# Six full-precision weight pieces of layer 0 turned into two-part pieces: ScalarE makes the high part and its negative, a DMA adds the weights

## The chip, the cores and the metric

One core of a Trainium2 chip runs the whole program. The metric is the device time of one execution in microseconds (us). The matrix engine is TensorE (PE in the profile; its weight loads are PEld), the elementwise engines are VectorE (DVE), ScalarE (ACT) and GpSimd (POOL), and SyncE (SP) issues most of the transfers.

## The reference

Two layers act on a sequence of 256 tokens with 1024 features, all in float32. Each layer is

```
mod = silu(c) @ w_mod[layer] + b_mod[layer]
shift, scale, gate = split(mod, 3)
hdn = rms_norm(x, norm_w) * (1 + scale) + shift
q1, k1, v1, g1, q2, k2, v2, g2 = split(hdn @ w_in[layer], 8)     # 8 x 512 columns
layer 0: y1 = diff_attention(q1, k1, v1),  y2 = dilated_attention(q2, k2, v2)
layer 1: y1 = moba_attention(q1, k1, v1),  y2 = stick_breaking_attention(q2, k2, v2)
x = x + gate * (concat(y1 * silu(g1), y2 * silu(g2)) @ w_out[layer])
```

The big products are `hdn @ w_in` (1024 x 4096) and `y @ w_out` (1024 x 1024) for each layer. `w_mod` (1024 x 3072 for each layer) is applied to one vector.

## The kernel before

**Pieces and steps.** Every 512-column group of `w_in` and `w_out` (K1, Q1, V1, K2, Q2, V2, G1, G2, O0, O1) is cut into four pieces of 256 rows, each a tile of 128 x 1024 floats (512 KB). There are 80 pieces, numbered in the order in which TensorE first needs them. TensorE's program is a list of 160 steps, 80 for a layer. A step multiplies one piece with one half of the tokens (or one half of the columns, for G1 and G2), so in layer 0 piece 20 (V2) is used in steps 40 and 41, 21 in 42 and 43, 22 in 44 and 45, 23 in 46 and 47, and pieces 24 to 27 (G1) in steps 48 to 55. `FIRST[n]` and `LAST[n]` are a piece's first and last step. After a step's projection TensorE does the attention work written down for it: scores of a pair of heads (pair 0 at step 27, then 31, 35, 39, and 46, 50, ...), transposes through the PSUM bank `turned`, products into the bank `mixed`. Each of these two banks is reused only when ACT or DVE has copied the last result out of it (`turn_act`, `mix_act`).

**Split and plain pieces.** Most pieces are split: ACT copies the loaded tile `raw` into `w_hi` as fp32r (`split_hi`, L478), DVE subtracts to get `w_lo` (`split_lo`, L751), and TensorE does three fp32r products (`mm3`: hi x hi, hi x lo, lo x hi). Pieces in the list `PLAIN` are multiplied as float32 straight from `raw`, with no work on ACT or DVE; the compiler turns each such product into two matmul instructions. A step of a split 512-column piece is thus 6 matmul instructions and one of a plain piece 4. For G1 and G2 they are 12 and 8, of 256 columns.

**Order on ACT and DVE.** Both engines walk the same 160 steps in program order. In a step g, ACT first copies what was turned or mixed in step g-1 (`take_turned`, L537 and L548; `take_mixed`, L561), then does the exponentials of the score maps (`exp_map`, L581: head 0 of a pair one step after the scores, head 1 two steps after), then the squares of finished tiles (L615) and the norm seeds (L467 to L471), and last the `split_hi` of the pieces whose `hi_at` is this step. DVE in step g does the masked logits (L853, one step after the scores), `normalise` (L865 to L876, head 1 three steps after the scores), the squares' sums (L890), `norm_tiles` (L916), then `split_lo` of the pieces with `hi_at(n) + 1 == g`, and then `take_mod` (L771), which multiplies a tile of `w_mod` with `c`; one each at steps 25, 26, 28, 29, 30, 33, 35, 37, 38, 41, 42, 43, ....

**Transfers.** SP issues the loads of pieces and `w_mod` tiles in one list, sorted by the step in which they are wanted (`FIRST[n]` for a plain piece, `hi_at(n)` for a split one). They go through a ring of seven `raw` tiles, and load i is issued when load i-7 has been used up: after `take_mod` for a `w_mod` tile, after `split_lo` for a split piece, after `LAST[n]` for a plain one. `w_hi` and `w_lo` are rings of eight slots over the split pieces alone. GpSimd makes bias maps from step 44 on and issues the loads of four late plain pieces (`HELD`) into `qT` and `kT`.

Of the kernel before, what the change touches and what calls it, by code (L numbers as in the profile page):

```python
# [9 lines left out]
ALU = mybir.AluOpType  # L10
ACT = mybir.ActivationFunctionType
# [22 lines left out]
STEPS = 80  # L34
# [33 lines left out]

HELD = (34, 37, 38, 39)
HELD_FROM = 59  # L70
PLAIN = (18, 19, 20, 21, 22, 23, 25, 26, 34, 37, 38, 39)
SPLIT = [n for n in range(len(FIRST)) if n not in PLAIN]


def split_before(n):

    i = SPLIT.index(n) - PIECES
    return SPLIT[i] if i >= 0 else None


def slot(n):
    return SPLIT.index(n) % PIECES


def split_count(n):
    return SPLIT.index(n) + 1


def done_at(layer, c, side):
# [29 lines left out]
def hi_at(n):  # L119
    if n < 12:  # L120
        return FIRST[n] - 6
    return CHANGE_HI.get(n, max(FIRST[n] - EARLY.get(n, 8), LAST[split_before(n)] + 1))


# [4 lines left out]
def lo_at(n):  # L129

    return hi_at(n) + 1


def pieces_lo(layer, g):
    return [n for n in SPLIT if lo_at(n) == STEPS * layer + g]

# [163 lines left out]
def program(nc, x, w_mod, w, a_lambda, vectors, consts, out):  # L302
    with ExitStack() as ctx:
# [6 lines left out]
        def sem(name):  # L310
            return ctx.enter_context(nc.semaphore(name))

        raw = sb("raw", [P, RAW, 2, CH])
        w_hi = sb("w_hi", [P, PIECES, 2, CH], F32R)
        w_lo = sb("w_lo", [P, PIECES, 2, CH], F32R)
# [61 lines left out]
        hi_done, lo_done, step_ok = sem("hi_done"), sem("lo_done"), sem("step_ok")  # L377
# [16 lines left out]
        y_ok, y_hi_ok, y_lo_ok = sem("y_ok"), sem("y_hi_ok"), sem("y_lo_ok")  # L394
        upd, out_ok, stored = sem("upd"), sem("out_ok"), sem("stored")
        dve_step = sem("dve_step")
        held_in = [sem(f"held_in{i}") for i in range(len(HELD))]


# [11 lines left out]
        def raw_tile(key):  # L411
            if key[0] == "w" and key[1] in HELD:
                return held[HELD.index(key[1])]
            return raw[:, place[key] % RAW, :, :]

        def wait_raw(eng, key):
            if key[0] == "w" and key[1] in HELD:
                return eng.wait_ge(held_in[HELD.index(key[1])], 16)
            eng.wait_ge(raw_full[place[key] % RAW], 16 * (place[key] // RAW + 1))

        def wait_step(eng, at):
            eng.wait_ge(step_ok, at + 1)
# [9 lines left out]
        @block.sync  # L432
        def _(sp):
            sp.dma_start(rows[:, :], vectors).then_inc(vec_in, 16)
            sp.dma_start(cst[:, C_ID:C_ID + P], consts[:, C_ID:C_ID + P]).then_inc(id_in, 16)
            sp.dma_start(xs[:, :, :], x[0].rearrange("(t p) f -> p t f", p=P)).then_inc(x_in, 16)
            for i, key in enumerate(loads):
                if i >= RAW:
                    was = loads[i - RAW]
                    if was[0] == "mod":  # L440
                        sp.wait_ge(mod_done, mods.index(was[1]) + 1)
                    else:
                        n = was[1]
                        if n in PLAIN:
                            wait_step(sp, LAST[n])
                        else:
                            sp.wait_ge(lo_done, split_count(n))
                whence = w_mod[mods.index(key[1])] if key[0] == "mod" else w[key[1]]
                sp.dma_start(raw_tile(key), whence.rearrange("p (k n) -> p k n", k=2)).then_inc(raw_full[i % RAW], 16)  # L449
                if key == ("w", 2):  # L450
                    sp.dma_start(lam, a_lambda.rearrange("a i d -> a (i d)").broadcast_to([P, 4 * HD])
                                 .rearrange("p (i d) -> p i d", i=4)).then_inc(lam_in, 16)
                if key == ("w", 11):
                    sp.dma_start(cst[:, C_TRI:], consts[:, C_TRI:]).then_inc(cst_in, 16)
            for i, (t, c) in enumerate((t, c) for t in range(2) for c in range(2)):
                sp.wait_ge(out_ok, i + 1)
                sp.dma_start(out[0, t * P:(t + 1) * P, c * CH:(c + 1) * CH],
                             xs[:, t, c * CH:(c + 1) * CH]).then_inc(stored, 16)
            sp.wait_ge(stored, 64)

        @block.scalar
        def _(act):
# [10 lines left out]
            def split_hi(n):  # L473

                wait_raw(act, ("w", n))
                if split_before(n) is not None:
                    wait_step(act, LAST[split_before(n)])
                nc.scalar.activation(w_hi[:, slot(n), :, :], raw_tile(("w", n)), ACT.Copy).then_inc(hi_done, 1)  # L478

            def h_hi(n, blocks, ts):  # L480

# [149 lines left out]
            for layer in range(LAYERS):  # L631
                for g in range(STEPS):
# [8 lines left out]
                    if at in X_SQUARE:  # L641
                        k = X_SQUARE.index(at)
# [4 lines left out]
                    for t in range(2):  # L647
# [4 lines left out]
                        if at == X_AT[t] + 1:  # L652
# [3 lines left out]
                            for kk in range(4):  # L656
                                k = 4 + kk
# [403 lines left out]

        @block.gpsimd
        def _(pool):
            pool.wait_ge(cst_in, 16)
            wait_turned(pool, ("qk", 0, Q2, 1))
            for M in range(8, 16):
                if M >= 12:
                    pool.wait_ge(logit_ok, M - 3)
                b = bias[:, M % 4, :]
                nc.gpsimd.tensor_scalar(b, dist, slope(M // 2, M % 2), 0.0, ALU.mult, ALU.add).then_inc(bias_a, 1)  # L1070
                pool.wait_ge(bias_a, M - 7)
                nc.gpsimd.tensor_tensor(b, b, dilated, ALU.add).then_inc(bias_ok, 1)


            wait_step(pool, HELD_FROM)
            for i, n in enumerate(HELD):
                nc.gpsimd.dma_start(held[i], w[n].rearrange("p (k n) -> p k n", k=2)).then_inc(held_in[i], 16)

        @block.tensor
        def _(pe):  # L1080
# [170 lines left out]
            def project(layer, g):  # L1251

                at = STEPS * layer + g
                c, p, s = STEP[layer][g]
                n = PIECE[layer, c, p]
                plain = n in PLAIN
                if plain:
                    full = raw_tile(("w", n))
                else:
                    wh, wl = w_hi[:, slot(n), :, :], w_lo[:, slot(n), :, :]  # L1260
                if layer == 0 and c == K1 and s == 0:
                    pe.wait_ge(h_ok, p + 1)
                if layer == 1 and c == K1 and p in (0, 2):
                    pe.wait_ge(h_ok, 5 + 2 * s + p // 2)
                if c >= O0 and plain:
                    pe.wait_ge(y_ok, 4 * layer + p + 1)
                elif c >= O0:
                    pe.wait_ge(y_lo_ok, 2 * layer + p + 1)
                if at == FIRST[n]:
                    if plain:  # L1270
                        wait_raw(pe, ("w", n))
                    else:
                        pe.wait_ge(lo_done, split_count(n))
                if p == 0:
                    was = before_in_bank(layer, c, s)
                    if was:
                        freed = free_act if freed_by_scalar(was[0], was[1]) else free_dve
                        if normed(*was[:2]):
                            pe.wait_ge(qn_ok, PARTS[NORMS.index(was[:2])] - 1 + s)
                        else:  # L1280
                            pe.wait_ge(freed, frees(*was))
                    if c == O1:
                        if layer == 0:
                            pe.wait_ge(logit_ok, 16)
                        else:
                            pe.wait_ge(d_a, 8)
                b = bank_of(layer, c, s)
                for a in range(2 if by_columns(layer, c) else 1):
                    for kk in range(2):
                        k = 2 * p + kk  # L1290
                        start, stop = k == 0 and a == 0, k == KB - 1
                        hb = k if c < O0 or k >= 4 else 8 + k
                        if by_columns(layer, c):
                            f = slice(2 * P * s + P * a, 2 * P * s + P * a + P)
                            i = mm(b[:, a * S:(a + 1) * S], full[:, kk, f], y[:, k, :], start, stop) if plain else mm3(b[:, a * S:(a + 1) * S], wh[:, kk, f], wl[:, kk, f],
                                    hy_hi[:, hb, :], hy_lo[:, hb, :], start, stop)
                        else:
                            ts = slice(s * P, s * P + P)
                            i = mm(b[:, :], y[:, k, ts], full[:, kk, :], start, stop) if plain else mm3(b[:, :], hy_hi[:, hb, ts], hy_lo[:, hb, ts], wh[:, kk, :], wl[:, kk, :], start, stop)
                i.then_inc(step_ok, 1)  # L1300
# [6 lines left out]
            for half in range(2):  # L1307
                for i in range(4):
                    m = V_CACT + 4 * half + i
# [107 lines left out]
```

## Time and profile before

| | |
|---|---|
| median of 3 runs | 325.1 us (324.76 to 325.23) |
| the profiled execution's own time | 324.23 us |
| its span in the profile | 322.4 us |
| granted TensorE clock, mean | 0.997 |
| TensorE busy | 299.4 us, 93% |
| VectorE busy | 235.2 us, 73% |
| ScalarE busy | 196.9 us, 61% |
| GpSimd busy | 16.2 us, 5% |
| read from HBM | 68.95 MB |

Busy times are sums over the span, and the share of a stage can be far from the mean. The time of an execution is some 1.8 us longer than the span, since it holds what lies before the first and after the last instruction.

### The profile page before, as it was taken

The numbers are of one execution on the slowest core, as the hardware profiler recorded it, in microseconds if no ns is written. First come the engines' busy times: TensorE is split into PE (matmuls) and PEld (weight loads), VectorE is DVE, ScalarE is ACT, GpSimd is POOL, SyncE is SP. The second block draws the span as 40 slices with busy tenths as digits, with TensorE's granted clock in tenths as the row PEclk, the third lists the DMA queues.
The fourth block names the chain that finished last, engine by engine and source line by source line (L and its number), as shares of the span: only waits on it lengthen the run. The fifth ranks groups of instructions, "written<-read, shape, count | busy, mean of one in ns | idle before, by whom it ended". The sixth has DMA issues, their size and how long they took to land.

```text
span 322.4 us, 4790 instructions
## 1 busy us (share of the span) xinstructions
PE 299.4 (93%) x1709; PEld 237.6 (74%) x1709; DVE 235.2 (73%) x480; ACT 196.9 (61%) x401; POOL 16.2 (5%) x24
## 2 busy tenths in 40 slices
PE   3498998999998999989999999999999999899995
PEld 2476876777555688886576888888987799798783
DVE  3898999998886697698957457989773547638633
ACT  3625568736745687998256446556664798959400
POOL 0000000000000942020000000000000000000000
PEclk9999999999999999999999999999999999999998
DMA  7999999495678958688752315679547148000011
GB/s 253 363 401 411 405 406 399 147 328 180 248 265 255 332 203 317 216 329 320 260 196 65 133 65 195 209 256 305 209 155 277 48 143 273 23 0 2 0 67 65
DMA packets 19879, 70.31 MB, mean 218 GB/s; under 512 B 2192, under 2 KB 2576, under 8 KB 19856
## 3 DMA queue, kind: packets, MB, share of 16 engines
q1 hardware_dynamic: 19280, 67.91, 58.4%
q0 software_dynamic: 576, 2.10, 1.7%
q8 instruction: 14, 0.23, 0.3%
q14 instruction: 9, 0.07, 0.1%
HBM read 68.95 MB, written 1.05 MB: 217 GB/s over the span
## 4 chain that ended last, share of the span: by engine, by line
PE 68%; DVE 12%; ACT 9%; DMA 5%; issue 3%; SPq 1%; ACTq 0%; DVEq 0%
PE proj L1082 46%; PE score L1082 13%; DMA raw<-in_w 5%; PE mixed L1082 5%; DVE raw L771 4%; DVE w_lo L751 3%; PE turned L1127 2%; ACT w_hi L478 2%; PE turned L1109 2%; DVE y L946 1%; DVE gt L938 1%; DVE probs L1021 1%; ACT y L502 1%; ACT gt L627 1%; SPq L449 1%
## 5 line engine op out<-in xcount | busy, mean ns | idle before, releaser
L751 DVE TENSOR_TENSOR w_lo<-raw,w_hi 128x1024 fp32r<-128x1024 f32 x68 | 82.3, 1222 | 14.1 <-ACT w_hi L478 13.6
L478 ACT ACTIVATE w_hi<-raw 128x1024 fp32r<-128x1024 f32 x68 | 70.6, 1050 | 17.8 <-DMA raw<-in_w 16.7
L1082 PE MATMUL proj<-w_hi,hy_hi 128*128 128x512 f32 x144 | 60.0, 417 | 4.8 <-DVE hy_lo L805 4.4
L771 DVE CUSTOM_DVE_ANT_0 raw<-raw,c_rows 128x1024 f32<-128x1024 f32 x48 | 59.0, 1251 | 0.0
L1082 PE MATMUL proj<-w_lo,hy_hi 128*128 128x512 f32 x144 | 56.9, 395 | 0.0
L1082 PE MATMUL proj<-w_hi,hy_lo 128*128 128x512 f32 x144 | 56.8, 394 | 0.0
L1082 PE MATMUL proj<-hy_hi,w_hi 128*128 128x256 f32 x176 | 52.5, 298 | 0.0
L1082 PE MATMUL proj<-hy_lo,w_hi 128*128 128x256 f32 x176 | 49.7, 283 | 0.0
L1082 PE MATMUL proj<-hy_hi,w_lo 128*128 128x256 f32 x176 | 49.7, 283 | 0.0
L1082 PEld LDWEIGHTS proj<-w_hi,hy_hi 128*128 128x128 f32 x144 | 27.5, 191 | 13.0 <-issue 3.9
L1082 PEld LDWEIGHTS proj<-hy_hi,w_hi 128*128 128x128 f32 x176 | 33.6, 191 | 2.1 <-issue 2.1
L1082 PEld LDWEIGHTS proj<-hy_lo,w_hi 128*128 128x128 f32 x176 | 33.6, 191 | 0.2 <-issue 0.2
L1082 PEld LDWEIGHTS proj<-hy_hi,w_lo 128*128 128x128 f32 x176 | 33.6, 191 | 0.0
L1082 PEld LDWEIGHTS proj<-w_hi,hy_lo 128*128 128x128 f32 x144 | 27.5, 191 | 6.1
L1082 PEld LDWEIGHTS proj<-w_lo,hy_hi 128*128 128x128 f32 x144 | 27.6, 191 | 5.4 <-issue 0.5
L581 ACT ACTIVATE probs<-logits,stat 128x128 f32<-128x128 f32 (+1 forms) x48 | 21.3, 446 | 6.7 <-DVE stat L853 6.7
L1082 PE MATMUL proj<-raw,y 128*128 128x512 f32 x48 | 22.4, 595 | 0.0
L548 ACT ACTIVATE probsT<-turned 128x384 f32<-128x384 f32 x20 | 9.7, 483 | 17.9 <-PE turned L1127 17.9
L890 DVE TENSOR_REDUCE n_ms<-sq 128x8 f32<-128x512 f32 (+1 forms) x13 | 9.4, 726 | 11.3 <-ACT sq L615 9.8
L1021 DVE SCALAR_TENSOR_TENSOR probs<-score,logits 128x384 f32<-128x384 f32 x8 | 4.1, 552 | 17.0 <-ACT logits L692 17.0
L1082 PE MATMUL score<-w_hi,hy_hi 128*128 128x512 f32 x40 | 16.1, 402 | 0.0
L1082 PE MATMUL score<-w_lo,hy_hi 128*128 128x512 f32 x40 | 15.6, 390 | 0.0
(147 smaller groups left out, 439.8 us busy)
## 6 DMA issues: line engine op xcount, KB each, us to landing
raw<-in_w SPq DMA_DIRECT2D x76, 512.0 KB, 4.7
raw<-in_w_mod SPq DMA_DIRECT2D x48, 512.0 KB, 5.7
xs<-in_x SPq DMA_DIRECT2D x1, 1024.0 KB, 5.2
qT<-in_w POOLq DMA_DIRECT2D x2, 512.0 KB, 6.5
kT<-in_w POOLq DMA_DIRECT2D x2, 512.0 KB, 8.4
out_x<-xs SPq DMA_DIRECT2D x4, 256.0 KB, 2.0
cst<-in_constants SPq DMA_DIRECT2D x1, 520.0 KB, 6.3
logits<-in_a_lambda SPq DMA_DIRECT2D x1, 128.0 KB, 12.1
```

Source lines behind the costliest of these rows:

```text
L449: sp.dma_start(raw_tile(key), whence.rearrange("p (k n) -> p k n", k=2)).then_inc(raw_full[i % RAW], 16)
L478: nc.scalar.activation(w_hi[:, slot(n), :, :], raw_tile(("w", n)), ACT.Copy).then_inc(hi_done, 1)
L502: j = nc.scalar.activation(y[:, k, :], b[:, i * S:(i + 1) * S], ACT.Identity, scale=v[:, V_A + k:V_A + k + 1], bias=v[:, V_B + k:V_B + k + 1])
L548: nc.scalar.activation(probsT[:, (2 * j + o) % 4, :], turned[:, 0:MAPW], ACT.Copy).then_inc(turn_act, 1)
L581: i = nc.scalar.activation(probs[:, M % 4, cs], logits[:, M % 2, cs], ACT.Exp, scale=-1.0, bias=st[:, tile:tile + 1], accum_out=st[:, 2 + ...
L751: nc.vector.tensor_tensor(w_lo[:, slot(n), :, :], raw_tile(("w", n)), w_hi[:, slot(n), :, :], ALU.subtract).then_inc(lo_done, 1)
L771: nc.vector.tensor_tensor_reduce(out=tile, in0=tile, in1=c_rows[:, :], scale=1.0, scalar=0.0, op0=ALU.mult, op1=ALU.add, accum_out=col(V_M ...
L890: nc.vector.reduce_sum(n_ms[:, n % 2, heads * s:heads * s + heads], src.rearrange("p (h d) -> p h d", h=heads), axis=AX.X).then_inc(ms_ok, 1)
L1021: nc.vector.scalar_tensor_tensor(out=probs[:, (2 * i + o) % 4, :], in0=score[o][:, 0:MAPW], scalar=0.0, in1=logits[:, o, :], op0=ALU.max, ...
L1082: return nc.tensor.matmul(o, a, b, start=start, stop=stop, skip_group_check=True)
L1109: i = nc.tensor.transpose(turned[:, b * P:(b + 1) * P], qn[:, s, b * P:(b + 1) * P], ident)
L1127: i = nc.tensor.transpose(turned[:, b * P:(b + 1) * P], probs[:, (2 * j + o) % 4, b * P:(b + 1) * P], ident)
```

## The change

Pieces 20 to 23 (V2) and 25, 26 (G1) of layer 0 leave `PLAIN` and become a third kind, `SUMMED`. ACT makes their `w_hi` as for a split piece, at the steps of `SUMMED_HI`, and right behind it, waiting for its own result, writes `w_lo = -w_hi` with a second pass. Then GpSimd issues a DMA that reads the piece from HBM again and adds it onto `w_lo`. DVE does nothing for these pieces. TensorE multiplies them with `mm3` after waiting for the adding DMA. SP frees their `raw` tile when `w_hi` is written. The load list is sorted by the new steps, and the slots of `w_hi` and `w_lo` move, since six more pieces pass through the ring of eight.

```
-PLAIN = (18, 19, 20, 21, 22, 23, 25, 26, 34, 37, 38, 39)
+PLAIN = (18, 19, 34, 37, 38, 39)
+
+SUMMED = (20, 21, 22, 23, 25, 26)
+SUMMED_HI = (28, 29, 31, 32, 35, 37)
 SPLIT = [n for n in range(len(FIRST)) if n not in PLAIN]
...
+def lo_count(n):
+
+    return sum(m not in SUMMED for m in SPLIT[:SPLIT.index(n) + 1])
...
+    if n in SUMMED:
+        return SUMMED_HI[SUMMED.index(n)]
...
 def pieces_lo(layer, g):
-    return [n for n in SPLIT if lo_at(n) == STEPS * layer + g]
+    return [n for n in SPLIT if n not in SUMMED and lo_at(n) == STEPS * layer + g]
...
+        neg_ok = sem("neg_ok")
+        summed_in = [sem(f"summed_in{i}") for i in range(len(SUMMED))]
...
                         if n in PLAIN:
                             wait_step(sp, LAST[n])
+                        elif n in SUMMED:
+                            sp.wait_ge(hi_done, split_count(n))
                         else:
-                            sp.wait_ge(lo_done, split_count(n))
+                            sp.wait_ge(lo_done, lo_count(n))
...
                 nc.scalar.activation(w_hi[:, slot(n), :, :], raw_tile(("w", n)), ACT.Copy).then_inc(hi_done, 1)
+                if n in SUMMED:
+                    act.wait_ge(hi_done, split_count(n))
+                    nc.scalar.activation(w_lo[:, slot(n), :, :], w_hi[:, slot(n), :, :], ACT.Copy,
+                                         scale=-1.0).then_inc(neg_ok, 1)
...
         @block.gpsimd
         def _(pool):
+            for i, n in enumerate(SUMMED):
+                pool.wait_ge(neg_ok, i + 1)
+                nc.gpsimd.dma_start(w_lo[:, slot(n), :, :], w[n].rearrange("p (k n) -> p k n", k=2),
+                                    accum_op=ALU.add).then_inc(summed_in[i], 16)
             pool.wait_ge(cst_in, 16)
...
                     if plain:
                         wait_raw(pe, ("w", n))
+                    elif n in SUMMED:
+                        pe.wait_ge(summed_in[SUMMED.index(n)], 16)
                     else:
-                        pe.wait_ge(lo_done, split_count(n))
+                        pe.wait_ge(lo_done, lo_count(n))
```

## Rows read from the trace of the kernel before

**Rows 1.** The profile's page: busy time of each engine; the chain by engine.
```profile
PE 299.4 (93%) x1709; PEld 237.6 (74%) x1709; DVE 235.2 (73%) x480; ACT 196.9 (61%) x401; POOL 16.2 (5%) x24
...
PE 68%; DVE 12%; ACT 9%; DMA 5%; issue 3%; SPq 1%; ACTq 0%; DVEq 0%
```

**Rows 2.** Busy time by stretch: us, busy of each engine, clock, DMA share, GB/s.
```profile
66.00:80.56 14.56, 14.56 (x79) 11.24 (x78) 12.87 (x41) 7.39 (x25) 0.00 (x0) 1.00 0.72 248
80.56:113.36 32.80, 31.93 (x147) 18.83 (x145) 24.13 (x66) 19.75 (x54) 8.64 (x12) 1.00 0.79 277
```

**Rows 3.** The chain of waits, stretch 66 to 126 us: start, us, what.
```profile
73.17 2.77 PE proj L1082 x12
...
85.70 3.44 PE proj L1082 x8
...
108.74 6.51 PE proj L1082 x36
...
116.58 1.73 PE proj L1082 x8
```

**Rows 4.** Timeline of ACT, steps 31 to 37: start, us, what, idle before.
```profile
70.52 0.60 ACT L615 ACTIVATE sq<-proj 128x512 f32<-128x512 f32 x1 [1.77 <-PE proj L1082]
73.21 0.49 ACT L548 ACTIVATE probsT<-turned 128x384 f32<-128x384 f32 x1 [2.09 <-PE turned L1127]
...
75.74 0.19 ACT L581 ACTIVATION_READ_ACCUMULATOR probs<-logits,stat 128x1 f32 x1
...
77.17 1.06 ACT L478 ACTIVATE w_hi<-raw 128x1024 fp32r<-128x1024 f32 x1
80.76 0.49 ACT L548 ACTIVATE probsT<-turned 128x384 f32<-128x384 f32 x1 [2.53 <-PE turned L1127]
82.58 0.40 ACT L581 ACTIVATE probs<-logits,stat 128x128 f32<-128x128 f32 x1 [1.33 <-DVE stat L853]
...
83.48 0.67 ACT L537 ACTIVATE kT<-turned,v 128x512 f32<-128x512 f32 x1
84.05 0.39 ACT L581 ACTIVATE probs<-logits,stat 128x128 f32<-128x128 f32 x1
```

**Rows 5.** Timeline of ACT at 113 us: one pass behind another.
```profile
113.36 1.04 ACT L478 ACTIVATE w_hi<-raw 128x1024 fp32r<-128x1024 f32 x1
114.30 1.48 ACT L590 ACTIVATE probs<-probs,stat 128x128 f32<-128x128 f32 x4
```

**Rows 6.** Timeline of DVE, steps 34 to 36.
```profile
76.90 0.16 DVE L870 RECIPROCAL stat<-stat 128x2 f32<-128x2 f32 x1
...
77.35 0.75 DVE L876 SCALAR_TENSOR_TENSOR probs<-probs,stat 128x128 f32<-128x128 f32 x2
...
81.91 0.29 DVE L853 CUSTOM_DVE_ANT_0 logits<-score,cst 128x128 f32<-128x128 f32 x1
```

**Rows 7.** Timeline of PE, steps 35 to 38.
```profile
80.17 0.55 PE L1127 MATMUL turned<-cst,probs 128*128 128x128 f32 x3
...
82.28 0.60 PE L1109 MATMUL turned<-cst,qn 128*128 128x128 f32 x4
...
85.54 3.60 PE L1082 MATMUL proj<-raw,y 128*128 128x512 f32 x8
```

**Rows 8.** Issue of piece 19's load; landing times of loads, 75 to 150 us.
```profile
72.04 0.33 SPq L449 DMA_DIRECT2D raw<-in_w  x1
...
DMA to landing us min/median/max: 3.2/4.4/7.9
...
kT<-in_w POOLq DMA_DIRECT2D x2, 512.0 KB, 8.4
```

**Rows 9.** Busy time in G2's stage; timelines of ACT and PE at step 53.
```profile
124.00:146.00 22.00, 20.22 (x167) 17.93 (x166) 16.63 (x42) 20.59 (x51) 2.30 (x4) 1.00 0.82 308
...
121.07 0.67 ACT L542 ACTIVATE y<-turned,v 128x512 f32<-128x512 f32 x1
...
122.37 0.60 PE L1119 MATMUL turned<-cst,gt 128*128 128x128 f32 x4
```

## The prediction

> **What bounds the kernel now.** I read the page first. TensorE is busy for 93% of the span and 68% of the chain that ended last is its own [rows 1], so a matmul saved on PE is worth its time wherever PE does not wait. Then I read the stretches. The six pieces are multiplied in steps 40 to 53, from about 90 to 122.4 us; the new ACT work is put at steps 28 to 37, from 66 to 84 us. In that earlier stretch PE is busy without a gap while ACT works for 7.39 of 14.56 us [rows 2]. The reader should see that this half-idle ACT is waiting for PE and DVE at fixed points, so that its free time is in the wrong places as much as in the right ones. Third I read the chain of waits for the price of a step, and last the timelines of ACT, DVE, PE and SP around steps 31 to 38, because what has to be known there is the order of the queues, which no sum shows.
>
> **What a step saves.** Two steps of split 512-column pieces take 2.77 us (12 instructions), two plain ones 3.44 us (8 instructions) [rows 3]. A split step is therefore 1.385 us and a plain one 1.72, and a V2 step saves 0.335 us. The eight V2 steps (40 to 47) give 2.7 us. A plain step of G1 takes 1.73 us; steps 47 to 50 take 6.51 together, of which 1.72 and 1.8 are the plain steps 47 and 50 (the second with 0.1 of hand-over to the scores behind it), so a split G1 step is about 1.49 [rows 3]. That saves 0.24 us in each of the steps 50 to 53, 1.0 us in all. PE's part is 3.7 us if nothing takes its place.
>
> **What of that ACT takes back later.** From the scores of step 46 on, ACT is nearly full: in G2's stage it works 20.59 of 22 us [rows 9]. It starts on the first subln tile at 121.07, after unbroken work, and PE can turn the second one into the same bank only when that copy ends, at 121.7; it does so at 122.37 today [rows 9]. So PE can come 0.6 us earlier here and no more, where steps 47 and 50 to 53 would give 1.3. What remains is 7 x 0.335 = 2.35 for steps 40 to 46 and 0.6, or 2.95 us. The bounds are 2.35 (ACT passes on nothing) and 3.7.
>
> **What the conversions cost before step 38.** One `w_hi` pass lasts 1.04 us and the next instruction may start 0.94 after it [rows 5]. The second pass waits for the first to end, so a piece costs ACT 1.06 + 0.94 and some 0.05 for the semaphore, 2.05 us; nothing in this trace shows a negating copy, and the same shape and engine give the price. Six pieces are 12.3 us. Followed through the queue:
>
> Steps 28, 29, 31 and 32 put four pieces (8.2 us) ahead of the exponentials of pair 1, head 1. ACT's idle time on that way is 1.77 + 2.09 us, and these exponentials end at 75.84 today (start of the last accumulator read 75.74 plus 0.1) [rows 4]. They end at 75.84 + 8.2 - 3.86 = 80.2. The scores of pair 0 are not hurt: head 1's exponentials end 2.1 us later, and the 1.1 us of `normalise` behind them still end before PE wants the map.
>
> DVE normalises pair 1 right behind: from 76.90 to 78.1 today [rows 6], so to 81.4. PE wants to turn this map at 80.17 [rows 7]. **First stall, 1.2 us.**
>
> ACT goes on with the norm seeds, a copy out of `mixed` and `w_hi` of piece 24, which today run from 75.84 to 78.1 [rows 4], so to 82.5; then piece 25 of step 35 (2.05), to 84.5. Only then does it copy the turned map of pair 1, which it started at 80.76 today. That copy frees the bank `turned` at 85.0. PE wants the bank for K2 at 82.28 [rows 7]. **The stall grows to 2.7 us in all.**
>
> DVE does `norm_tiles`, `split_lo` of piece 24, `take_mod` of step 35 and then the logits of pair 2: 5.0 us from 76.90 to 81.91 [rows 6]. Begun 3.3 us later, at 80.2, this brings the logits to 85.2 and those of head 0 to 85.8. ACT's exponentials (0.9) and the copy of K2's first half (0.57) follow [rows 4], so `turned` is free again at 87.3 to 87.4; PE wants it at 84.43, after one more step of 1.72. **The stall is 3.0 us** when step 38, today at 85.54, may start at 88.5.
>
> The load of piece 19, plain and needed in that step, is the last term. Today it is issued at 72.04 [rows 8], 13.5 us ahead, because its ring slot falls free at the `take_mod` of step 30. In the new list six pieces come earlier, and its slot is that of the `w_mod` tile of step 35, used up at 85.2. A load lands 3.2 to 7.9 us after its issue, 4.4 in the median [rows 8]: at 89.7 with the median, 1.2 us after PE could start. The range is 0 to 4.7. **By step 38 PE is 4.2 us late.** From there ACT has only pieces 26 and 27 in front of it, and its 13 idle us between 80.56 and 113.36 [rows 2] let it catch up before the turn of step 39; I add 0.2 for the shorter steps behind which the Q2 norm chain (43, 44) has to hide. The bounds of this part are 3.0 and 8.0; below 3.0 only if my order on ACT is wrong, and then down to 1.2, the first stall alone.
>
> **The other parts.** DVE loses nothing and gains nothing: plain pieces never used it. The adding DMAs follow the negating passes, which by the queue above end at about 70, 73, 75.5, 79, 84.5 and 90.3 us, and are read at steps 40 to 52, from 94 to 120 us. The nearest rows are the loads that GpSimd issues, 8.4 us to landing [rows 8]; even twice that is hidden for each. GpSimd does nothing else before step 44. They add 3.1 MB to a stretch that moves 248 GB/s with a DMA share of 0.72 [rows 2], beside 3.1 MB of loads pulled forward. I take their effect on pieces 18 and 19 as nothing beyond the median above; the upper bound is the 7.9 us. The ring tiles that come free sooner in steps 40 to 53 feed loads that already arrive in time, since PE waits for none today. POOL, PEld and the clock (1.00 in all these stretches [rows 2]) stay as they are.
>
> One rule speaks against the change and is not in the sum. In the Trainium skill, "Collectives: The Full Stack" (Part 3, the bandwidth ceiling) says that a DMA add is slowed by its two source reads, and so runs at about half the rate of a copy. No row here has an adding DMA. As an estimate by that page, each one would take the DMA engines as long as two loads.
>
> **The sum.** 4.2 + 0.2 - 2.95 = +1.45 us, on the profiled execution 324.23 + 1.45 = 325.7. The median of the runs shown is 0.9 above that execution, so 325.1 + 1.5 = 326.6 us.
>
> **The rivals.**
> *The gain comes through.* ACT's idle time absorbs the conversions, with only the first stall, 1.2 us, left: 325.1 + 1.2 - 2.95 to -3.7 is 322.6 to 323.4. For it speaks that ACT is half idle from 66 to 80 us; against it, that the order above puts 6.15 us of conversions between scores and exponentials of the same pair. This decides if the turn of K2 starts less than 1 us later after the turn of step 35 than now.
> *Piece 19 is in time.* The load lands in 3.2 us: 3.0 + 0.2 - 2.95 is +0.25, 325.4 us, no change. It needs a quiet queue, but an adding DMA (piece 25) and the load of piece 27 are issued within a microsecond of it.
> *The transfers become the bound.* Six adds and six earlier loads share the DMA engines in 68 to 92 us; piece 18 (issued about 74.5, needed at 81.7) and piece 19 land late together. With 7.9 us to landing for piece 19: 325.1 + 7.7 + 0.2 - 2.95 = 330.1, with 6 us 328.2. The stretch 80 to 113 already has a share of 0.79 [rows 2]. The half rate that the Trainium skill ("Collectives: The Full Stack") gives for adds would lead here; no row shows it.
> *The split products are no cheaper.* If three fp32r products took as long as one float32 product, the change would only cost: 325.1 + 4.2 + 0.2 = 329.5. For it speaks that a split step has 6 instructions and a plain one 4; the chain's durations [rows 3] speak plainly against it.
>
> **Numbers.** Forecast, 325.8 to 328.4: 0.45. Piece 19 in time, 324.5 to 325.7: 0.18. Gain comes through, below 324.4: 0.24. Transfers the bound, above 328.4: 0.11. No cheaper: 0.02. A difference under 0.2% (0.65 us) is about what a measurement here can't tell from none. Faster is 0.24, same 0.18, slower 0.58. The range 322.8 to 329.3 reaches into both outer rivals and leaves out their far ends, where ACT's order costs nothing (below 322.8, 0.07) or piece 19 lands after 7 us and more (above 329.3, 0.08, with the last rival); the forecast's own is 325.8 to 328.4.
>
> **What would show it.** PE's two-step stretch at V2 should fall from 3.44 to 2.77 us. PE's turn of pair 1's map should be released by DVE's L876, the turn of K2 by ACT's copy L548 and L537, and step 38 by the DMA of `raw`, issued behind the `take_mod` of step 35. ACT should be without a gap from 67 to about 92 us. I am wrong if PE has no idle time between 80 and 92 us, if piece 19's load is issued well before 85, or if G1's steps bring 0.24 each with ACT no obstacle.

## The result, and the profile after

The changed kernel takes 333.96 us in the median (333.43 to 335.36, 4 runs) against 324.93 us for the kernel before in the same session (324.39 to 325.23, 4 runs). The ratio is 1.0294 [1.0273, 1.0314]: 9 us slower. The forecast of 326.6 us had the direction and missed the size by 7.4 us; 333.96 is also above the range. The profiled execution has a span of 331.9 us, where the one before had 322.4.

The page of the changed kernel, to be laid beside [rows 1]. In the slices, each of 8.3 us, PEclk is the granted clock in tenths:

```profile
span 331.9 us, 4878 instructions
...
PE 297.7 (90%) x1741; PEld 241.0 (73%) x1741; DVE 235.4 (71%) x480; ACT 208.3 (63%) x413; POOL 21.5 (6%) x30
...
PEclk9997999999589999999999999999999999999999
...
q1 hardware_dynamic: 19280, 67.91, 56.6%
q0 software_dynamic: 1440, 5.24, 6.5%
...
PE 64%; ACT 12%; DMA 10%; DVE 9%; issue 4%; SPq 1%; ACTq 0%; DVEq 0%
...
w_lo<-in_w POOLq DMA_DIRECT2D x6, 512.0 KB, 9.6
```

PE is busy for 1.7 us less than before (297.7 against 299.4), and yet the span grows by 9.5. The DMA's share of the chain has doubled, from 5 to 10%, and two slices of the clock, at about 83 to 99 us, have fallen to 0.5 and 0.8. Both point to one place. (The 0.7 at 25 to 33 us, behind a wait of 2.66 us for DVE, costs nothing: the turn that PE began at 60.08 us before begins at 60.12.) PE's timeline there:

```profile
81.36 0.55 PE L1149 MATMUL turned<-cst,probs 128*128 128x128 f32 x3 [0.95 <-DVE probs L894]
90.56 3.53 PE L1104 MATMUL proj<-raw,y 128*128 128x512 f32 x4 [8.66 <-DMA raw<-in_w]
93.93 0.60 PE L1131 MATMUL turned<-cst,qn 128*128 128x128 f32 x4
```

The first line is the predicted turn of pair 1's map (before at 80.17 [rows 7]), 1.2 us late. The second is step 36, the first of the plain piece 18: PE waits 8.66 us for that load. The third shows that the step then took 3.37 us (90.56 to 93.93) where a plain step takes 1.72. The windows say why, and what the DMA engines did meanwhile (columns as in [rows 2]):

```profile
66.00:78.00 12.00, 12.00 (x63) 9.31 (x60) 8.45 (x31) 10.96 (x22) 2.77 (x3) 1.00 0.97 298
78.00:82.00 4.00, 2.95 (x18) 1.77 (x16) 2.84 (x9) 3.90 (x12) 0.88 (x1) 1.00 1.06 278
82.00:86.00 4.00, 0.00 (x0) 0.00 (x0) 4.00 (x12) 2.30 (x4) 0.00 (x0) 0.68 1.06 278
86.00:90.00 4.00, 0.00 (x0) 0.00 (x0) 1.88 (x6) 1.29 (x6) 0.87 (x1) 0.50 1.03 284
90.00:94.00 4.00, 3.44 (x5) 1.47 (x6) 0.00 (x0) 0.00 (x0) 0.00 (x0) 0.54 1.06 285
94.00:98.00 4.00, 4.00 (x21) 2.58 (x20) 1.77 (x5) 3.40 (x7) 0.00 (x0) 1.00 1.03 418
```

The last two columns are to be read together. From 66 us on all 16 DMA engines are full (shares of 0.97 to 1.06, where [rows 2] have 0.72 and 0.79), but while adds are in flight they move only 278 to 298 GB/s; when the fifth is through (it lands at 94.7) they move 418 GB/s at the same share. Full engines that move less: the adds cost engine time that their bytes don't show. The clock column is 0.50 in the second half of the wait and 0.54 in the step behind it, which is the 1.2 GHz level, and 1.00 (2.4 GHz) from 94 us on.

The chain of waits from 72 to 94 us, where before it ran through PE (the 2.77 and 3.44 us pieces of [rows 3]):

```profile
73.38 0.96 ACT w_hi L492
74.33 0.02 issue
74.35 16.17 DMA raw<-in_w
90.52 0.04 issue
90.56 3.53 PE proj L1104 x4
```

Piece 18 is issued at 74.35, as the prediction had it (about 74.5), and takes 16.17 us to land, where a load took 3.2 to 7.9 before [rows 8]. POOL's timeline shows what ran beside it, and the tile's view gives the landing times:

```profile
70.29 1.03 POOL L1084 DMA_DIRECT2D w_lo<-in_w  x1 [69.84 <-ACT w_lo L495]
73.21 0.88 POOL L1084 DMA_DIRECT2D w_lo<-in_w  x1 [1.88 <-ACT w_lo L495]
75.71 0.86 POOL L1084 DMA_DIRECT2D w_lo<-in_w  x1 [1.62 <-ACT w_lo L495]
79.48 0.88 POOL L1084 DMA_DIRECT2D w_lo<-in_w  x1 [2.92 <-ACT w_lo L495]
86.33 0.87 POOL L1084 DMA_DIRECT2D w_lo<-in_w  x1 [5.97 <-ACT w_lo L495]
```
```profile
L1084 POOL DMA_DIRECT2D w_lo<-in_w x6: 857/870/1033, 70.3 to 98.5; - x6
...
DMA to landing us min/median/max: 8.4/9.6/11.2
```

The adds themselves land in 8.4 to 11.2 us, long before their readers want them. It is the ordinary load beside them that comes late.

**Where the 9.5 us are.** The scores of pair 3 (step 39) and of step 46 are good milestones: 89.07 and 107.81 before, 100.72 and 117.28 after. At the first PE is 11.65 us behind: 0.95 for the turn, 8.66 for the load, 1.65 for the clock, and 0.4 for an earlier offset and hand-overs. Between the two it takes 16.56 us instead of 18.74, so the split products give back 2.2. From step 46's scores to the end it is 214.6 us in both (322.4 - 107.81 and 331.9 - 117.28): the split G1 steps bring nothing.

### The profile page after: what moved, and what is told of

Its sections match the earlier page's. It is cut to its first block, busy times and chain, and to the rows that moved or that the text cites. A ratio compares the mean times of both kernels' runs of the same rounds, so it can differ in the third digit from the quotient of the medians.

```text
span 331.9 us, 4878 instructions
## 1 busy us (share of the span) xinstructions
PE 297.7 (90%) x1741; PEld 241.0 (73%) x1741; DVE 235.4 (71%) x480; ACT 208.3 (63%) x413; POOL 21.5 (6%) x30
## 3 DMA queue, kind: packets, MB, share of 16 engines
q1 hardware_dynamic: 19280, 67.91, 56.6%
## 4 chain that ended last, share of the span: by engine, by line
PE 64%; ACT 12%; DMA 10%; DVE 9%; issue 4%; SPq 1%; ACTq 0%; DVEq 0%
PE proj L1104 43%; PE score L1104 13%; DMA raw<-in_w 10%; PE mixed L1104 5%; ACT w_hi L492 2%; PE turned L1131 2%; DVE raw L789 2%; PE turned L1149 2%; DVE w_lo L769 1%; ACT probs L599 1%; DVE y L964 1%; DVE gt L956 1%; DVE logits L871 1%; DVE probs L1039 1%; ACT y L520 1%
## 5 line engine op out<-in xcount | busy, mean ns | idle before, releaser
L492 ACT ACTIVATE w_hi<-raw 128x1024 fp32r<-128x1024 f32 x74 | 76.8, 1050 | 18.4 <-DMA raw<-in_w 17.1
L1104 PE MATMUL proj<-w_hi,hy_hi 128*128 128x512 f32 x160 | 66.7, 417 | 5.3 <-DVE hy_lo L823 5.0
L1104 PE MATMUL proj<-w_hi,hy_lo 128*128 128x512 f32 x160 | 63.1, 394 | 0.0
L1104 PE MATMUL proj<-w_lo,hy_hi 128*128 128x512 f32 x160 | 63.1, 394 | 0.0
L1104 PE MATMUL proj<-hy_hi,w_hi 128*128 128x256 f32 x192 | 56.8, 296 | 0.0
L1104 PE MATMUL proj<-hy_lo,w_hi 128*128 128x256 f32 x192 | 54.2, 282 | 0.0
L1104 PE MATMUL proj<-hy_hi,w_lo 128*128 128x256 f32 x192 | 54.2, 282 | 0.0
L1104 PEld LDWEIGHTS proj<-w_hi,hy_hi 128*128 128x128 f32 x160 | 30.5, 190 | 13.6 <-issue 4.3
L1104 PE MATMUL proj<-raw,y 128*128 128x512 f32 x16 | 9.0, 704 | 8.7 <-DMA raw<-in_w 8.7
L1104 PE MATMUL score<-w_hi,hy_lo 128*128 128x512 f32 x40 | 15.6, 390 | 0.0
```

Source lines behind the costliest of these rows:

```text
L1104: return nc.tensor.matmul(o, a, b, start=start, stop=stop, skip_group_check=True)
```

## The experiments

The question was which of these holds the loss: what an adding DMA costs beyond a copy, the mere bytes of six more reads, ACT's queue, the order of the loads, or the clock. The median of the kernel before was 324.89 us beside the first four experiments, 324.5 beside the next four and 324.19 beside the last two; each ratio is against its own. The diffs are against the changed kernel unless said otherwise.

**1. The same DMAs as plain copies.** The low part is then the whole weight, and the kernel leaves out the subtraction.
```diff
-  nc.gpsimd.dma_start(w_lo[...], w[n]..., accum_op=ALU.add).then_inc(summed_in[i], 16)
+  nc.gpsimd.dma_start(w_lo[...], w[n]...).then_inc(summed_in[i], 16)
```


> The changed kernel with the six adding DMAs turned into plain copies of the same bytes from the same queue to the same place (the low part then holds the whole weight, so the sum of the products is another one). Theory A, an add occupies the DMA engines about twice as long as a copy, and that work is what makes piece 18 land 16.2 us after its issue: the work outstanding between 68.6 and 90.5 us falls from about 3.1 MB of loads + 2 x 2.1 MB of adds to 3.1 + 2.1 MB, 13 us at 400 GB/s, so piece 18 lands at 81 to 84 us, PE waits 0 to 2 us instead of 8.7, and the median is 325.5 to 328.5 us. Rival B, it is the number of transfers and bytes, whatever they do: piece 18 still lands after 88 us, and the median stays above 332 us. Rival C, the passes on ACT are the cost: no change from the changed kernel, 334 us.

Measured: 329.77 us, ratio 1.0148 [1.0106, 1.019], above the expected 325.5 to 328.5 and below rival B's 332. PE's wait for piece 18 is halved, not gone:

```profile
86.67 3.78 PE L1103 MATMUL proj<-raw,y 128*128 128x512 f32 x4 [4.02 <-DMA raw<-in_w]
```

The DMA engines are as full as with the adds, but now move 410 GB/s (columns as in [rows 2]):

```profile
82.00:86.00 4.00, 0.55 (x3) 0.31 (x3) 3.93 (x9) 3.34 (x5) 0.53 (x1) 0.89 1.07 410
```

The page gives the cost of a DMA in engine time:

```profile
q0 software_dynamic: 1440, 5.24, 4.3%
```

That queue also carries the four held loads, which the kernel before has alone at 1.7% of 322.4 us: 5.5 us of all 16 engines, 1.37 each. Six copies take 4.3% of 328.8 less 5.5, so 1.44 us each; six adds take 6.5% of 331.9 less 5.5, so 2.68 us each. An add costs 1.9 times a copy of the same 512 KB. So about half of the wait is what the adds cost beyond copies (8.66 against 4.02 us), and the other half comes with six plain copies in their place. The expectation that took the dearer add for the whole cause was wrong.

The rule that the prediction had set beside its sum stands in the Trainium skill, "Collectives: The Full Stack", Part 3, the bandwidth ceiling: the reducing step of a collective needs two source reads for its DMA add and runs at about half the rate of the copying one. The page speaks of rings of cores, not of a load; this trace agrees with the ratio, 2.68 against 1.44 us. That a second read is the reason here too was not tried.

**2. No adding DMAs at all.** PE waits for the negative high part alone, and the kernel leaves out the weights' part of `w_lo`.
```diff
-  nc.gpsimd.dma_start(w_lo[...], w[n]..., accum_op=ALU.add).then_inc(summed_in[i], 16)
...
-  pe.wait_ge(summed_in[SUMMED.index(n)], 16)
+  pe.wait_ge(neg_ok, SUMMED.index(n) + 1)
```


> The changed kernel without the six adding DMAs: PE waits for the negating pass instead (the low part is then the negative high part alone). Theory A: the wait for piece 18 is gone. What remains is the ACT queue: first stall 1.0 us, 2.7 by the turn of K2, 3.0 by step 38, then the wait for piece 19, 0 to 1.5 us, and against it 2.2 to 2.95 us saved at steps 40 to 53: 325.4 to 327.0 us. Rival B, the six loads pulled forward are themselves too much before step 36: PE still waits more than 2 us for piece 18, median above 328 us. Rival C, ACT: 334 us.

Measured: 326.49 us, ratio 1.0049 [1.0032, 1.0066]; the span is 323.9. PE's idle times:

```profile
81.43 0.55 PE L1147 MATMUL turned<-cst,probs 128*128 128x128 f32 x3 [0.95 <-DVE probs L894]
...
84.84 0.63 PE L1129 MATMUL turned<-cst,qn 128*128 128x128 f32 x4 [1.15 <-ACT probsT L566]
...
87.56 0.63 PE L1129 MATMUL turned<-cst,qn 128*128 128x128 f32 x4 [0.37 <-ACT kT L555]
...
88.69 3.62 PE L1102 MATMUL proj<-raw,y 128*128 128x512 f32 x8
```

These are the three stalls that the prediction worked out, at the predicted instructions: 1.2, 2.7 and 3.0 us had been forecast as running totals, and PE starts step 38 at 88.69, which had been put at 88.5. There is no wait for a load: piece 19 is issued at 85.30 (predicted 85.2) and is there 3.3 us later, at 88.6, just as PE wants it. So the conversions on ACT cost 3.2 us at the scores of pair 3 (92.24 against 89.07), the loads pulled forward cost nothing without the adds, and 1.6 us come back by the scores of step 46 (109.42 against 107.81). The transfers of the adds are worth 333.96 - 326.49 = 7.5 us.

**3. The adds held back until steps 34, 36, 38, 40, 41 and 42,** so that piece 18 goes ahead of most of them.
```diff
   pool.wait_ge(neg_ok, i + 1)
+  wait_step(pool, ADD_FROM[i])
```


> The changed kernel with the same work, but GpSimd issues the adds only when PE has done steps 34, 36, 38, 40, 41 and 42. Theory A: piece 18 (issued at 74.4) lands by 80 us as no add is in flight, PE's wait of 8.7 us and the 1.65 us lost to the lower clock behind it go away; piece 19 (issued at 85.2) then shares the queues with two adds and lands 5 to 8 us later, a wait of 1.5 to 4.5 us: 327 to 330 us. Rival D, the adds move the stall to where they are read: PE waits for an add at step 40 or 42 by 2 us or more, and the median stays above 330 us. Rival C, ACT: 334 us.

Measured: 331.94 us, ratio 1.0229 [1.0188, 1.0269], above the expected 327 to 330, which had no term for the clock. Piece 18 is now in time and piece 19, 6.9 us to landing, is not:

```profile
92.01 6.65 PE L1106 MATMUL proj<-raw,y 128*128 128x512 f32 x8 [3.42 <-DMA raw<-in_w]
```

Two plain steps take 6.65 us, where [rows 3] have 3.44 for them: the clock is 0.50 to 0.64 between 90 and 98 us. The wait costs 3.4 us and the clock behind it 3.2. The DMA share is 1.02 to 1.11 from 86 to 98 us: the surplus of work was moved, and only in part taken away.

**4. The six pieces split in the ordinary way,** at the same steps, the low part by DVE, without an adding DMA.
```diff
-SUMMED = (20, 21, 22, 23, 25, 26)
-SUMMED_HI = (28, 29, 31, 32, 35, 37)
+SUMMED = ()
+SUMMED_HI = ()
...
+ 20: 28, 21: 29, 22: 31, 23: 32, 25: 35, 26: 37   (added to CHANGE_HI)
```


> The six pieces as ordinary split pieces at the same steps: one ACT pass each, the low part by DVE one step later, no add. Theory A plus my account of the ACT queue: ACT has four passes (3.9 us) instead of eight ahead of the exponentials of pair 1, head 1, which its idle 3.9 us absorb, but DVE gets six passes of 1.14 us, three of them before its normalise of step 34; DVE has only 2.3 us idle from 64 to 82 us. First stall 0.5 to 2 us, piece 19 issued 2 to 4 us late but landing in time or by 1 us late, gain at steps 40 to 53 of 2.2 to 2.95: 323.5 to 326 us. Rival C (ACT passes were the whole cost, six instead of twelve): about half the loss, 329 us. Rival E (DVE becomes the bound): above 327 us.

Measured: 326.78 us, ratio 1.006 [1.0043, 1.0076].

```profile
82.77 0.55 PE L1150 MATMUL turned<-cst,probs 128*128 128x128 f32 x3 [2.40 <-DVE probs L895]
```

DVE is the queue that is late here: PE waits 2.40 us for it, the clock averages 0.79 from 82 to 90 us, and by the scores of pair 3 PE is 4.5 us behind (93.57). Both the wait (expected 0.5 to 2 us) and the time (323.5 to 326) came out higher than expected. It is still 7 us faster than the changed kernel. Against experiment 2, where ACT makes both passes and nothing is added, it is 0.3 us slower, and the two intervals overlap: to spare DVE the low parts was worth no more than that, and was paid for with 7.5 us of transfers.

**5. The adds alone.** The kernel before, plus six adding DMAs into slots of `w_lo` that are idle and are overwritten before their next use, at steps 28 to 37. The diff is against the kernel before.
```diff
+ EXTRA = ((20, 2, 28), (21, 3, 29), (22, 4, 31), (23, 5, 32), (25, 6, 35), (26, 7, 37))
...
+ for i, (n, s, at) in enumerate(EXTRA):
+     wait_step(pool, at)
+     nc.gpsimd.dma_start(w_lo[:, s, :, :], w[n]..., accum_op=ALU.add).then_inc(extra_in[i], 16)
```


> The kernel before, with nothing changed but six adding DMAs of the same six pieces, issued by GpSimd when PE has done steps 28, 29, 31, 32, 35 and 37, into w_lo slots that hold nothing then (DVE waits for them before it writes the slot). Order and steps of all other loads are those of before, with pieces 18 and 19 issued at 68.6 and 72.0 us. Theory A': the adds cost only where a load wanted soon stands behind them; piece 18 lands before the first adds take effect and piece 19 (needed at 85.5) has 13 us, so PE waits 0 to 1 us and the median is 324.9 to 326.5 us. Rival G: the volume of the adds alone (six times two loads' work) starves PE wherever the loads stand: a wait of more than 3 us on a load, median above 328.

Measured: 330.99 us, ratio 1.0217 [1.0197, 1.0237]. Nothing else of the change is in this kernel, and it has 6.5 us of the loss, where 0 to 1.5 were expected; rival G, the volume of the adds alone, was right. Pieces 18 and 19, issued early, are in time; the wait is at piece 20, issued at 82.5 and 11.7 us to landing:

```profile
94.27 5.40 PE L1091 MATMUL proj<-raw,y 128*128 128x512 f32 x8 [3.68 <-DMA raw<-in_w]
```

Up to the scores of pair 3 this kernel is level with the one before (89.18 against 89.07); 3.68 us of wait and 2.0 us of a slower pair of steps (5.40 against 3.44) are all of the 5.7 us by which its span is longer.

**6. Only the V2 pieces;** 25 and 26 stay plain, so four adds.
```diff
-PLAIN = (18, 19, 34, 37, 38, 39)
+PLAIN = (18, 19, 25, 26, 34, 37, 38, 39)
-SUMMED = (20, 21, 22, 23, 25, 26)
+SUMMED = (20, 21, 22, 23)
-SUMMED_HI = (28, 29, 31, 32, 35, 37)
+SUMMED_HI = (28, 29, 31, 32)
```


> The changed kernel with only the four V2 pieces (20 to 23) as summed pieces, and the two G1 pieces (25, 26) plain as before. If the two G1 pieces bring nothing at steps 50 to 53 because ACT sets the pace from step 46 on (PE in the second run gained 1.6 us from scores of step 39 to those of 46 and lost 0 from there to step 53), nothing is lost by leaving them out, and two ACT passes of 2.05 us, two adds and two early loads go: piece 18 stands one load earlier (issued at 73.2) and the wait for it falls from 8.7 to 3 to 6 us; the second and third stall (copy of the turned map behind piece 25) go. 328 to 331 us. If the G1 steps did bring their 1.0 us: the time between the turns of steps 50 and 53 grows by 1 us against the changed kernel. Rival B', the adds of pieces 20 to 23 alone already hold piece 18 to 90 us: median 333 or more.

Measured: 330.87 us, ratio 1.0203 [1.0184, 1.0222], in the expected range (328 to 331).

```profile
87.00 3.78 PE L1104 MATMUL proj<-raw,y 128*128 128x512 f32 x4 [4.14 <-DMA raw<-in_w]
```

Dropping the fifth and sixth piece takes 4.5 us off the wait for piece 18; with them go the fifth add and the load of piece 25 ahead of piece 18, and what each is worth was not tried apart. It loses nothing in G1: from the scores of step 46 (114.49) to the end it takes 329.0 - 114.49 = 214.5 us, with plain G1 steps, where the changed kernel takes 214.6 with split ones.

**7. The four V2 pieces split late,** at steps 34, 35, 38 and 39, in the ordinary way, with 24 and 27 moved behind them. Against the kernel before:
```diff
-PLAIN = (18, 19, 20, 21, 22, 23, 25, 26, 34, 37, 38, 39)
+PLAIN = (18, 19, 25, 26, 34, 37, 38, 39)
...
+ 20: 34, 21: 35, 22: 38, 23: 39, 24: 41, 27: 42   (added to CHANGE_HI)
```


> A candidate from these readings: the kernel before with the four V2 pieces as ordinary split pieces (low part by DVE, no add), converted where ACT and DVE have idle time: 20 at step 34, 21 at 35, 22 at 38, 23 at 39, and pieces 24 and 27, which stood at 34 and 38, at 41 and 42; G1 stays plain. Theory A: no adds, no load order that puts six pieces ahead of 18 and 19 (issued at about 70 and 78 us); PE loses 0 to 0.5 us before step 40 and keeps 1.6 to 2.0 us of V2: 323.0 to 324.3 us against 324.9. Rival E (DVE is late): DVE gets three more passes between steps 39 and 45 and PE is 2 us faster there, 5.4 us against 5.9 us idle; if it comes late with the logits of step 47, the gain is given back: 324.9 to 326.

Measured: 324.65 us, ratio 0.9998 [0.998, 1.0015], where 323.0 to 324.3 had been expected. This trace starts 0.6 us later than that of before (its first scores are at 65.88 against 65.24). With this taken off, no stall has come up by the scores of pair 3 and PE is 1.8 us ahead at step 46 (106.69). Then:

```profile
115.95 0.55 PE L1128 MATMUL turned<-cst,probs 128*128 128x128 f32 x3 [1.29 <-ACT probs L591]
```

PE waits for a map that ACT scales, and at the end all 1.8 us are gone: from the scores of step 46 it takes 216.3 us here (323.0 - 106.69), 214.6 in the kernel before. A gain on PE counts up to the place where the chain of ACT and DVE begins to set the pace; pieces 24 and 27, moved into it, are the likely load, which was not tried apart.

**8. Piece 18's load moved forward** in the order of the loads.
```diff
-later = [(FIRST[n] if n in PLAIN else hi_at(n), 1, ("w", n)) ...
+later = [(34 if n == 18 else FIRST[n] if n in PLAIN else hi_at(n), 1, ("w", n)) ...
```


> The changed kernel with one load moved: piece 18 is issued ahead of pieces 24 and 25 and one w_mod tile, at about 70 us instead of 74.4. Work and adds are the same. Theory A (the DMA engines have more work than time between 69 and 92 us): piece 18 lands in time, before 81 us, but pieces 24 and 25 land later, 25 at 86 to 89 us, and ACT, which converts 25 ahead of its copy of the turned map, holds PE at the turn of K2 (step 36) instead; the loss moves and shrinks little: 330 to 334 us. Rival F, only the place of piece 18 in the queue is wrong: PE waits for nothing but the three ACT stalls (2.5 us) and piece 19: 326.5 to 328.5 us.

Measured: 334.23 us, ratio 1.0295 [1.0275, 1.0315], the same as the change (expected were 330 to 334). Piece 18 is in time, but now ACT waits for the pieces it has to convert, and PE behind ACT:

```profile
84.99 1.06 ACT L492 ACTIVATE w_hi<-raw 128x1024 fp32r<-128x1024 f32 x1 [2.91 <-DMA raw<-in_w]
...
88.80 1.06 ACT L492 ACTIVATE w_hi<-raw 128x1024 fp32r<-128x1024 f32 x1 [2.75 <-DMA raw<-in_w]
```
```profile
91.47 1.08 PE L1131 MATMUL turned<-cst,qn 128*128 128x128 f32 x4 [7.03 <-ACT probsT L566]
```

So it was not the place of piece 18 in the list: with the DMA engines full (a share of 1.02 to 1.08 from 80 to 96 us), this order only changes who waits.

**9. Experiment 7, with the low parts of 20 to 23 made by GpSimd.** Against the kernel before, beside the edits of experiment 7:
```diff
+BY_POOL = (20, 21, 22, 23)
...
+ for n in BY_POOL:
+     pool.wait_ge(hi_done, split_count(n))
+     nc.gpsimd.tensor_tensor(w_lo[:, slot(n), :, :], raw_tile(("w", n)),
+                             w_hi[:, slot(n), :, :], ALU.subtract).then_inc(pool_lo, 1)
```


> The late-split candidate (V2 pieces 20 to 23 split at steps 34, 35, 38, 39) with their low part made by GpSimd, idle there, instead of DVE. In the candidate before, PE was 1.7 us ahead at the scores of step 46, but DVE, full from 97 to 110 us, had their logits no earlier (109.6), and all was given back. Theory A+E (pace from step 46 on is set by DVE and ACT, not PE): with three passes of 1.14 us fewer on DVE in that stretch the logits follow the scores, and 1.2 to 1.7 us stay: 322.9 to 323.8 us against 324.6. Rival H, GpSimd and DVE slow each other (DVE passes of 1.75 instead of 1.22 us beside GpSimd in the kernel before) and a subtraction takes GpSimd over 5 us, so DVE is as late as it was: 324.3 to 325.5 us.

Measured: 323.08 us, ratio 0.9947 [0.9928, 0.9966], 1.1 us (0.5%) faster than the kernel before, the best of all, and inside the expected range. POOL's timeline:

```profile
79.57 5.67 POOL L1076 TENSOR_TENSOR w_lo<-raw,w_hi 128x1024 fp32r<-128x1024 f32 x2 [79.12 <-ACT w_hi L488]
88.64 4.71 POOL L1076 TENSOR_TENSOR w_lo<-raw,w_hi 128x1024 fp32r<-128x1024 f32 x2 [3.40 <-ACT w_hi L488]
```

Two passes take 4.7 to 5.7 us, twice DVE's 1.22 us each, on an engine that did nothing before step 44. No bytes are added. The second subln turn is at 122.14 in a trace that starts 1.26 us late, so at 120.9 on the old scale, against 122.37 [rows 9]: 1.5 us survive where experiment 7 kept none.

**10. Only pieces 20 and 21 split, at steps 34 and 35,** in the ordinary way, with 24 and 27 moved to 38 and 41, against the kernel before.
```diff
-PLAIN = (18, 19, 20, 21, 22, 23, 25, 26, 34, 37, 38, 39)
+PLAIN = (18, 19, 22, 23, 25, 26, 34, 37, 38, 39)
...
+ 20: 34, 21: 35, 24: 38, 27: 41   (added to CHANGE_HI)
```


> Only pieces 20 and 21 as ordinary split pieces, at steps 34 and 35, with 24 and 27 moved to 38 and 41; low parts by DVE. PE's direct saving is four steps of 0.335, 1.3 us, and DVE has two passes more, one of them after step 39. Theory A+E: DVE's slack of some 3.6 us before step 46 takes them, 0.8 to 1.3 us stay: 323.4 to 324.0 us. If the passes of DVE eat it as with four pieces: 324.5 us.

Measured: 323.69 us, ratio 0.9975 [0.9964, 0.9987]: 0.5 us faster, a small difference, as expected (323.4 to 324.0). By the scores of step 46 PE is 0.9 us ahead on the old scale (107.92 in a trace that starts 1.0 late), and from there to the end it takes the usual 214.6: with half the conversions nothing is given back.

## Why the prediction was wrong

**The step that failed** is this one, about the adding DMAs: "I take their effect on pieces 18 and 19 as nothing beyond the median above; the upper bound is the 7.9 us." It gave a load 4.4 us to landing, and at most 7.9; piece 18 took 16.17. That term was 0 for piece 18 and measured 8.66 us of wait, plus 1.65 us for the step that then ran at the low clock. Removing the adds (experiment 2) takes 7.5 us off the time, and the adds put into the old kernel (experiment 5) bring 6.5 us on: shown from both sides.

The mistake was one of method. The prediction compared landing times with due times, add by add, and never summed the engine time of all transfers in the stretch. The rows for it were there. [rows 2] leave (1 - 0.72) x 14.56 = 4.1 us of idle DMA time from 66 to 80.56, and at 0.79 another 2.1 us up to 90.5: 6 us. The held loads stood on the page at 1.37 us of all 16 engines each, so as copies the five adds issued by then were 6.9 us, already over 6, and the loads pulled forward come on top. Where the shares would pass 1, some load has to be late. At 2.68 us the four adds issued by 79.5 are 10.7 us. The six loads that SP issues from 68.64 to 74.35, piece 18 the last, are 8.7 us at 1.45 each (56.6% of 331.9 us for 67.91 MB). Together that is 19.4 of the 21.9 us between 68.6 and 90.5, and the fifth add and later loads were in flight beside them. This last sum is a reading of the shares, not an experiment of its own.

**The rival was named and held too small.** "The transfers become the bound" had the right pieces and the right issue time of piece 18, but only 0.11 and a worst case of 330.1 us, because it took its worst landing time, 7.9 us, from rows with DMA shares of 0.72 and 0.79. (By its own terms 6 us to landing give 328.05 us, not 328.2, which changes nothing.) The rule of the half rate was left out of the sum, and the rival kept a chance of 0.11.

**ACT's queue** was right. The exponentials of pair 1, head 1 end at about 80.0 (predicted 80.2); two passes cost 2.05 us a piece:

```profile
67.83 1.05 ACT L492 ACTIVATE w_hi<-raw 128x1024 fp32r<-128x1024 f32 x1
68.92 1.06 ACT L495 ACTIVATE w_lo<-w_hi 128x1024 fp32r<-128x1024 f32 x1
69.88 0.38 ACT L599 ACTIVATE probs<-logits,stat 128x128 f32<-128x128 f32 x1
...
79.88 0.19 ACT L599 ACTIVATION_READ_ACCUMULATOR probs<-logits,stat 128x1 f32 x1
```

The turn of pair 1's map was forecast for 81.4 and came at 81.36. In the changed kernel ACT too waited for a late load (1.67 us for piece 25, up to 83.89), under cover of PE's longer wait; no term of the forecast had that. Experiment 2, which is the change without its transfers, takes 326.49 us; the forecast was 326.6. That it fits so well is partly luck: two terms that were too high, a cost and a gain, nearly cancel. They follow.

**Piece 19's wait** of 1.2 us did not come: in experiment 2 the load is there after 3.3 us, near the 3.2 us end of [rows 8]. In the changed kernel it took 11.7 us (issued at 85.22), and PE, late by then, didn't have to wait for it.

**The gain** was too high. A V2 step did save what the chain said (two steps in 2.77 us, the last line below), but steps 40 to 46 kept 2.2 us in the changed kernel and 1.6 in experiment 2, for the 2.35 forecast, and G1 kept 0 for 0.6. From the scores of step 46 to the end, ten of the twelve kernels, with plain and with split G1 steps, take 214.5 to 214.6 us each; the two that come there earliest take longer (216.3 and 215.0, experiments 7 and 9). Where before the chain in this part was PE's up to 126 us [rows 3], in the changed kernel it leaves PE at 113.9 and runs through ACT's and DVE's work on other pieces:

```profile
114.52 1.06 ACT w_hi L492
...
116.75 1.56 DVE raw L789
...
118.73 0.34 DVE logits L871
```

So PE no longer sets the pace there; which of these instructions would have to go to let the gain through was not tried.

The price of a V2 step, for comparison:

```profile
102.13 2.77 PE proj L1104 x12
```

**The other rivals** fell: the gain did not come through, since ACT's order cost what it was said to cost, and the split products are cheaper, as the line above shows.

**The clock** was said to stay as it is. It fell during the long wait, and the step behind it took 3.37 us. No experiment held the clock up through such a wait; the lengths of steps at either level are the evidence.

## What to carry to other kernels

Before transfers are added or moved, sum the engine time of everything that will be in flight in that stretch, and compare it with the idle part of the DMA share; landing times read from a stretch with idle engines don't hold once that sum passes the time there is, and an adding DMA counted as 1.9 copies here. Where the DMA engines are nearly full, a re-read from HBM is a price even as a plain copy (329.77 against 326.49 us). A conversion from data already on the chip, placed later and on an engine that is idle (GpSimd here), beat both kernels. And a saved PE step is worth its time only up to the next place where another engine's chain sets the pace.

## What the runs showed of the hardware

- An adding DMA from HBM of 512 KB (128 rows of 4 KB) takes 2.68 us of all 16 DMA engines, a copy by the same queue 1.44. The same working gives 2.6 for the four adds of experiment 6 (4.8% of 329.0 less 5.5, over 4), and 2.6, 2.6 and 2.9 for experiments 5, 8 and 3. To landing it is 8.4/9.6/11.2 us (least, median, most) against 6.1/7.6/8.1 for the copies of experiment 1.
- A long PE wait costs twice. Behind waits of 3.4 to 8.7 us the next step or two ran at a granted clock of 0.50 to 0.64: one step in 3.37 us for 1.72, two in 6.65 for 3.44. Behind the 2.40 us of experiment 4 the clock averaged 0.79. In experiment 2, with idle times of 1.15 us and less, two steps took 3.62 and the clock stood at 1.00. Waits of 2.0 to 2.8 us went either way: early in the kernel (17 to 33 us) the clock behind 1.98, 2.66, 2.67 and 2.75 us was 0.57 to 0.64 (experiment 7, the changed kernel, experiments 10 and 2), behind 2.22 and 2.45 us 1.00 (the kernel before, experiment 1).
- Subtractions on GpSimd (128x1024, two inputs) took 2.4 to 2.8 us each, for 1.22 on DVE.
